# A hybrid decoder layer in split fp32r products: the hi and lo parts of each activation row moved side by side

## The reference, cut to what matters

```
h = x + 1/2 * SwiGLU_a(RMSNorm(x))                  # width 2816
u = RMSNorm(h);  P = u @ W_in                       # 16 blocks of 128 columns, and a rank-16 gate
    gated linear attention (4 heads), S5 state space mixer (32 groups)
h = h + concat(GLA out, S5 out) @ W_out
h = h + CrossAttn(RMSNorm(h), memory K/V)           # W_q, W_kv, W_o
h = h + 1/2 * SwiGLU_b(RMSNorm(h))
y = RMSNorm(h)
```

## Time and profile before

| what | value |
|---|---|
| median of 3 runs | 1285.82 us |
| span of the profiled execution | 1282.0 us |
| the runs' median less that span | 3.8 us |
| TensorE matmuls | 10151 of them, busy 1261.7 us, 98% |
| VectorE, ScalarE, GpSimd busy | 857.1, 531.3, 353.9 us |
| chain that ended last | TensorE 92% |
| DMA | 129.94 MB, mean 101 GB/s |

### The profile page before, as it was taken

The page is one execution under the profiler, slowest core; times in us unless marked ns, Lnnn a source line. Parts: engine busy times, 40 slices in busy tenths (PEclk is TensorE's granted clock), DMA queues, the critical chain, the costliest instruction groups (busy, mean ns, idle before and its releaser), DMA issues.

```text
span 1282.0 us, 24086 instructions
## 1 busy us (share of the span) xinstructions
PE 1261.7 (98%) x10151; PEld 1218.5 (95%) x10151; DVE 857.1 (67%) x1061; ACT 531.3 (41%) x803; POOL 353.9 (28%) x411
## 2 busy tenths in 40 slices
PE   7999999999999999999999999999999999999997
PEld 6999999999999999999899997599999999999997
DVE  4986479847885636558565437479995589637953
ACT  6644145511224422574443324246553255414543
POOL 0026723288893201000002100032330133102321
PEclk9999999999999999999999999999999999999999
DMA  6233323263223442125333756322332323323322
GB/s 182 81 96 90 91 85 99 83 137 91 74 65 94 91 81 65 51 69 154 119 89 93 232 197 223 122 83 66 100 99 83 99 83 99 91 83 91 87 63 74
DMA packets 221084, 129.94 MB, mean 101 GB/s; under 512 B 22256, under 2 KB 213280, under 8 KB 220960
## 3 DMA queue, kind: packets, MB, share of 16 engines
q1 hardware_dynamic: 217024, 123.83, 33.8%
q10 hardware_dynamic: 3952, 4.58, 1.1%
HBM read 121.42 MB, written 5.78 MB: 99 GB/s over the span
## 4 chain that ended last, share of the span: by engine, by line
PE 92%; DVE 4%; ACT 2%; issue 1%; DMA 1%; SPq 0%; ACTq 0%; DVEq 0%
PE PS L736 89%; PE PS L1361 1%; DMA AR<-in_x_prompt 1%; PE PS L806 0%; ACT wh L1500 0%; ACT gua L1649 0%; DVE Hs L2452 0%; DVE xl L2139 0%; PE PS L1338 0%; DVE AR L2780 0%; PE PS L953 0%; PE PS L1447 0%; DVE ARr L2134 0%; DVE yl L2233 0%; DVE wl L2027 0%
## 5 line engine op out<-in xcount | busy, mean ns | idle before, releaser
L1500 ACT ACTIVATE wh<-raw 128x1024 fp32r<-128x1024 f32 (+1 forms) x126 | 130.1, 1032 | 373.7 <-PE PS L736 373.1
L736 PE MATMUL PS<-yh,wh 128*128 128x288 f32 x960 | 205.6, 296 | 0.0
L736 PE MATMUL PS<-yl,wh 128*128 128x288 f32 x960 | 204.7, 295 | 0.0
L736 PE MATMUL PS<-yh,wl 128*128 128x288 f32 x960 | 204.6, 295 | 0.0
L2027 DVE TENSOR_TENSOR wl<-raw,wh 128x1024 fp32r<-128x1024 f32 (+1 forms) x126 | 154.9, 1229 | 63.7 <-ACT wh L1500 62.3
L736 PE MATMUL PS<-xh,ARr 128*128 128x288 f32 x792 | 174.1, 297 | 0.4 <-ACT sq L1583 0.2
L736 PE MATMUL PS<-xh,wh 128*128 128x288 f32 x736 | 164.4, 305 | 0.1
L736 PE MATMUL PS<-xh,wl 128*128 128x288 f32 x736 | 158.1, 297 | 0.0
L736 PE MATMUL PS<-xl,wh 128*128 128x288 f32 x736 | 157.9, 296 | 0.0
L736 PEld LDWEIGHTS PS<-yh,wh 128*128 128x128 f32 x960 | 154.1, 189 | 1.5 <-DVE yl L2705 0.8
L736 PEld LDWEIGHTS PS<-yh,wl 128*128 128x128 f32 x960 | 154.3, 189 | 0.0
(11 more groups left out here) (378 smaller groups left out, 2183.5 us busy)
## 6 DMA issues: line engine op xcount, KB each, us to landing
raw<-in_w_ffn_gu SPq DMA_DIRECT2D x88, 512.0 KB, 3.9
raw<-in_w_ffn_down SPq DMA_DIRECT2D x32, 512.0 KB, 3.9
raw<-in_w_in SPq DMA_DIRECT2D x16, 512.0 KB, 4.0
raw<-in_w_ckv SPq DMA_DIRECT2D x16, 512.0 KB, 3.8
raw<-in_w_ffn_down SPq DMA_DIRECT2D x16, 384.0 KB, 3.4
Hs<-in_cache_mem_k SPq DMA_DIRECT2D x6, 1024.0 KB, 6.5
raw<-in_w_out SPq DMA_DIRECT2D x8, 512.0 KB, 4.0
raw<-in_w_cq SPq DMA_DIRECT2D x8, 512.0 KB, 4.3
```

What stands on the lines that cost most here:

```text
L736: return e.matmul(out, lhsT, rhs, start=start, stop=stop, **kw)
L1500: e.activation(wh[:, n % 2, 0:K * P], raw[:, n % 4, 0:K * P], ACT.Copy).then_inc(w_hi, 1)
```

## The change

The two parts become one tensor of 8 x 2 x 576, and `xh`, `xl` are strided views of it, so row k of `xl` starts 2,304 bytes behind row k of `xh`, right where row k of `xh` ends. The y pair is changed in the same way. The token sums are laid out by kind i, then row k, then part, so the low part starts 1,152 bytes behind the high one. `acc` (the sums of squares, 2,560 bytes) now lies ahead of `wh` and `wl`. Because rows of x now lie elsewhere in `Xs` and `Hs`, `osq` moves, `zT` moves to AR, and in the W_OUT group all sample states are computed at blocks 0 and 1 (eight instructions each) and written out before row 2. TensorE's program has the same instructions in the same order.

```diff
-        xh = sb("xh", [P, KD, T], F32R)
-        xl = sb("xl", [P, KD, T], F32R)
+        xx = sb("xx", [P, KD, 2, T], F32R)
+        xh, xl = xx[:, :, 0, :], xx[:, :, 1, :]
         Hs = alias("Hs", 2 * KD * T)
-        yh = sb("yh", [P, KD, T], F32R)
-        yl = sb("yl", [P, KD, T], F32R)
+        yx = sb("yx", [P, KD, 2, T], F32R)
+        yh, yl = yx[:, :, 0, :], yx[:, :, 1, :]
         raw = sb("raw", [P, 4, KD * P])
+        acc = sb("acc", [P, NT * P])
         wh = sb("wh", [P, 2, KD * P], F32R)
         wl = sb("wl", [P, 2, KD * P], F32R)
-        acc = sb("acc", [P, NT * P])
...
-        osq = view(Hs, 4608, 18, DV)
+        osq = view(Hs, 2 * T, 18, DV)
...
-        zT = view(Hs, 4608, 4, T)
+        zT = view(AR, 0, 4, T)
...
-        tok_h, tok_l = view(ARr, 0, HK, 4, TH), view(ARr, 8 * T, HK, 4, TH)
-        tok_hf, tok_f = tok_h.bitcast(F32), view(AR, 8 * T, HK, 4, TH)
+        tok_h, tok_l = (view(ARr, 0, 4, 2 * HK, TH).rearrange("p i (k s) t -> p k i s t", s=2)[:, :, :, s, :] for s in range(2))
+        tok_hf = tok_h.bitcast(F32)
+        tok_f = view(AR, 0, 4, 2 * HK, TH).rearrange("p i (k s) t -> p k i s t", s=2)[:, :, :, 1, :]
...
         def chunk(t, k):
-            return t[:, bass.ds(k, 1), :].rearrange("p a t -> p (a t)")
+            return t[:, k, :]
...
-                if k == 4:
+                if k == 2:
                     e.wait_ge(S("snew_ok"), 2 * NB)
                     for f in range(2):
                         e.dma_start(O["gla_s"][0, :, 2 * f:2 * f + 2].rearrange("b q d e -> (q d) b e"),
...
                 conv(n + 2)
-                if i < 4:
-                    sample_states(i)
+                if i < 2:
+                    sample_states(2 * i)
+                    sample_states(2 * i + 1)
                 e.wait_ge(ps_free, seq(n) + 3)
```

## The result

The changed kernel took 1288.92 us (median of 12 runs, 1287.68 to 1290.29), the kernel before, run beside it, 1286.07 us (median of 12). The ratio is 1.0027 with a 95% interval of 1.0019 to 1.0035: slower, by 2.85 us between the medians and by 3.5 us (2.4 to 4.5) by the ratio, which leaves out the one run of the kernel before that took 1918.52 us. The time lies inside the predicted range, but the case forecast as likeliest, no change, is not the one that came.

The account below looks back on a forecast made before the run. TensorE was taken as the bound, busy 1261.7 of 1282.0 us, so its matmul pace decides. Five terms of 0 on a 1282.0 us span, plus 3.8 us to the median, gave 1285.8 us; range 1276 to 1291.

Parts of the forecast that it names:

- no change: Whole kernel: the change does nothing to TensorE, time within 0.2% of before, 1283.3 to 1288.4 us; chance 0.45.
- Step 1: TensorE's matmuls, whose read addresses change: cost 0, bounds -16.6 to +5.2 us.
- high end: Upper bound for the matmuls: quick down groups +2.6 us and token-sum matmuls +2.6 us, together +5.2 us.
- The term for the tokens: 1584 matmuls on token sums go from 131.7 to 133.3 ns, +2.6 us.
- the other 2.6 us of that end: The two quick down groups of 384 matmuls fall to the slow pace, +2.6 us.
- The rival "slower": Token sums and the two quick down groups: layout puts all streams at the slow level, 1291.0 us; chance 0.22.
- Reading on without a jump is quicker: Dense blocks, step from high second half to low first half: 848 pairs quicker, -5.7 us, 1280.1 us; chance 0.18.
- the pace tips: Dense groups: three to all of the other 11.25 tip to the quick level, -3.9 to -14.6 us; chance 0.15.
- Steps 2 to 5: Sample states in W_OUT, their output on ScalarE's queue, moved scratch, strided token-sum pieces: each cost 0.

Follow-up runs that it names:

- e0: The kernel before, unchanged, run once more for a second trace; 1284.76 us (one run).
- e8: Kernel before with token sums ordered by kind, part, row (rows 1,152 bytes apart, low part 4,608 behind); 1282.79 us, ratio 0.9985.
- e11: Kernel before with the token order of e5 and the `mst` move of e6 together; 1281.15 us, ratio 0.9973.
- e2: The changed kernel with only the token sums' layout turned back to that of before; 1285.11 us, ratio 1.0002.
- e1: Kernel before with the token sums' new layout alone; 1288.48 us, ratio 1.0030.
- e9: Kernel before with the low part of the token sums 128 bytes further back, scratch behind it moved 256 bytes; 1288.89 us, ratio 1.0035.
- e3: Kernel before with `acc` ahead of `wh` and nothing else moved; 1285.14 us, ratio 1.0001.
- e4: Kernel before with token sums ordered by row, part, kind (rows 9,216 bytes apart, low part 4,608 behind); 1285.21 us, ratio 1.0001.
- e6: Kernel before with `mst` (96 bytes) put ahead of `h`, so x, y and weights start at multiples of 256 bytes; 1283.51 us, ratio 0.9992.
- e7: Kernel before with dense blocks' 576 token columns cut into 320 and 256 in place of 288 and 288; 1286.66 us, ratio 1.0014.
- e10: Kernel before with the low part of the token sums 256 bytes further back, scratch moved as in e9; 1284.81 us, ratio 1.0006.
- e5: Kernel before with token sums ordered by kind, part, row, the same kernel as e8; 1282.08 us (single run).

## Why the prediction was wrong

**The base of the sum.** The forecast stood on a span of 1282.0 us and a median 3.8 us above it, and took the 3.8 us for what lies around the span. In the runs since, a run is 1.8 us above its own span; the other 2.0 were luck of the profiled execution, which had two quick groups where e0 had one. That did no harm to the forecast, but it hid that the kernel before varies by several us (27 runs from 1283.31 to 1287.52 beside e8 to e11).

**Step 1, the matmuls: this failed.** It took 0 for all streams, because the rows of a down group and of gate/up blocks showed that jumps between the parts cost nothing. Those rows are of x and y, whose parts lay 18,432 bytes apart and now lie 2,304 apart, both multiples of 256. For them the 0 was right within what e2 can tell. But the token sums got another distance, 1,152 bytes, and no row bore on that. One value was taken for two edits. The sum of the working should have listed each stream's distances separately, and then the token layout would have stood out as the only one without a row.

Its high end was nearly the case that came. The term for the tokens, 2.6 us for 1584 matmuls, was meant as a fall from 131.7 to 133.3 ns. By the groups the two token groups of after are 2.4 and 1.1 us above those of e2, and the x products 0.7 below (173.6 against 174.3), so 2.8 us; from start to start the 33 units take 369.9 us before and 372.8 after. The size was right, by an accident of the bound: S1 and S2 fall to 134.7 and 135.4 ns, past the level of the x products, A22 and S3 only to 133.5.

**The lost quick groups, the other 2.6 us of that end.** Both are gone in the trace of after, but the kernel before loses one of them in e0 by itself. None is quick in the three traces with parts at two places (after, e1, e9); those with before's token places had 2 (before), 1 (e0), 1 (e2), 2 (e3), 0 (e4), 1 and most of the last group (e6), 0 (e7) and 0 (e10). The medians of e1 and e9 are 3.7 and 4.1 us above those of before, more than the 2.8 of the products, and one quick group is worth 1.3; that of after is 2.85 above (3.5 by the ratio). So the token layout may also keep groups from the quick level, and it isn't shown; three traces are too few, and their intervals take in 2.8. In the traced pair the sum is 2.8 + 2.6 = 5.4 us, against 4.5 of span. Of the rest, 0.9 us is an earlier start of everything in that one execution: the same pair of matmuls begins a product at 80.30 us before and at 79.37 after.

```profile
80.30 0.43 PE L736 MATMUL PS<-ARr,xh 128*128 128x288 f32 x2
```
```profile
79.37 0.83 PE L737 MATMUL PS<-ARr,xx 128*128 128x288 f32 x5
```

**The rival "slower".** It named the place, the token sums, and a price, and both held. The reason it gave, rows 2,304 bytes apart like those of x, did not: e9 has before's token rows, 4,608 bytes apart, and is slow, and in e2 the rows of x lie 4,608 bytes apart and its products are as in before. That x products pay 1.6 ns more was a true reading of the earlier trace rows with the wrong cause put to it: in A11 and A12 e6 takes it away without touching any distance. As its reason was weak, 0.22 was a fair chance for it; as one of two edits had no row, it deserved more.

**Reading on without a jump is quicker; the pace tips.** The first did not come: e2 has the new x and y layout, and its gate/up blocks have 482 matmuls in 64.00 us, as before. The second did not come by this change, but e8 shows that its mechanism exists: a token order that tips four stretches, 2.0 us off the median.

**Steps 2 to 5: right.** The sample states are covered as worked out; the first add waits for TensorE by 0.48 us, not by the 0.4 that 668.60 less 668.2 gave, which is close. The copies to the moved scratch and the token operations, groups by line, after:

```profile
L1792 ACT ACTIVATE AR<-PS 128x288 f32<-128x288 f32 x4 | 3.0, 741 | 1.9 <-PE PS L1019 1.9
L2469 DVE COPY AR<-PS 128x288 f32<-128x288 f32 x4 | 2.9, 722 | 6.1 <-PE PS L1019 6.0
L1579 ACT ACTIVATE ARr<-AR 128x864 fp32r<-128x864 f32 x8 | 7.3, 913 | 2.7 <-DVE AR L2162 2.7
L2149 DVE TENSOR_TENSOR ARr<-AR,ARr 128x864 fp32r<-128x864 f32 x8 | 8.4, 1051 | 0.0
```

741 and 722 ns against 738 and 718, 913 and 1051 against 913 and 1052.

**The pages.** By e10 and e9 the spacing of 288-column matmuls in S2 goes from 131.6 ns (1579/12) to 135.4 (1625/12) with nothing changed but where a read starts. The Trainium skill, "TensorE: Matmul & The Clock Gate", section "Back-to-back issue gap", says that in a stream of weight loads and matmuls both set the spacing, and gives N/2.4 + 2.5 ns for one isolated matmul, 122.5 ns at 288 columns. No level shown here is as quick as that (130.0 ns is the quickest for 288 columns), and the page does not name the place of an operand. "SBUF — State Buffer", section "Operand start alignment", in the Trainium skill asks only for a start at a multiple of the element size and says of itself that it is about legality and not speed; these runs show that speed is another matter.

## What to carry to other kernels

When a layout change is weighed, write down for each stream where its reads start modulo 256 bytes, before and after; a new distance without a row in the trace is an unknown with a cost of its own. In a kernel bound by the pace of TensorE, keep the parts that are streamed in turn at the same place modulo 256 bytes. Multiples of 256 were best for A11 and A12 here, by up to 1.9 ns a matmul; dense blocks gained nothing from them that shows outside one group. And where executions of one kernel differ by microseconds, look first at which of them the profile shows before its span is made the base of a sum.

## What the runs showed of the hardware

The distance from one matmul of 288 fp32r columns to the next depended, in the seven products, on where the streamed operand starts modulo 256 bytes. The start places follow from the layouts, the times from the table divided by 12:

| weights in | start places of the reads | ns | where |
|---|---|---|---|
| AR | all 0 | 131.5 to 131.7 | S1, S2 before; A11, A12 in e6 |
| AR | all 160 | 133.0 to 133.5 | A11, A12 before |
| AR | 0 and 128 in turn | 134.7 to 135.4 | S1, S2 after, and in e9 |
| x | all 128 | 131.8 to 131.9 | A22, S3 before |
| x | 0 and 128 in turn | 132.9 to 133.5 | A22, S3 after, and in e9 |

The granted clock is 1.00, 2.4 GHz, in every stretch shown. Only changes of place by 128 bytes and by multiples of 256 were tried in the token sums. The place is not all of it: S4 streams all its reads from 128 in e6 and has 133.0 ns there, where A22 and S3 have 131.4 to 131.7 from the same place with their weights elsewhere; and S4 goes from 134.0 in before to 133.2 in e1, though nothing of its own moved, only the token sums streamed ahead of it.

Dense blocks have two levels, 130.0 and 133.3 ns, held over four to eight blocks in a row and both seen with the same program. In every block with halves of 288 columns the two halves start 1,152 bytes apart, so at places 128 bytes apart. Pieces of 320 and 256 columns at one place gave no gain (e7); equal halves at one place weren't tried. What sets the level stays open: four stretches are quick in each of the three traces with one token order (e5, e8, e11), with before's order it differs from execution to execution, and in e6 a group turns quick at its second block.
